# Encoder trunk in split fp32 on one core: tokens as rows in chunks 1 to 10 of each feed-forward stage, and h turned by VectorE and a trip through scratch memory

## What is computed

```python
DEPTH = 2; SEQ = 256; D_MODEL = 1024; D_FF = 2816
def _swiglu(h, w_in, w_out):
    gu = h @ w_in                       # (256, 1024) @ (1024, 5632)
    gate, up = jnp.split(gu, 2, axis=-1)
    return (jax.nn.silu(gate) * up) @ w_out
for l in range(DEPTH):
    x = x + 0.5 * _swiglu(_rmsnorm(x, ffn1_norm[l]), ffn1_w_in[l], ffn1_w_out[l])
    x = x + mixing(_rmsnorm(x, mix_norm[l]))
    x = x + 0.5 * _swiglu(_rmsnorm(x, ffn2_norm[l]), ffn2_w_in[l], ffn2_w_out[l])
```

## Time and profile before

| | |
|---|---|
| median of 3 runs | 906.71 us |
| the profiled execution | 906.24 us, span 904.4 us |
| granted TensorE clock | 1.000 of full speed throughout |
| busy share of the span | TensorE 99%, VectorE 68%, ScalarE 53%, GpSimd 6% |
| DMA | 169.63 MB, mean 188 GB/s |

### The profile page before, as it was taken

How to read it: one execution, slowest core, us unless ns; L and a number is a source line. 1 busy time by engine, 2 the same in 40 slices (tenths; PEclk the granted TensorE clock), 3 DMA queues, 4 the chain that set the end, 5 groups by cost and what they waited for, 6 DMA issues and landing times.

```text
span 904.4 us, 13686 instructions
## 1 busy us (share of the span) xinstructions
PE 899.1 (99%) x4874; PEld 765.0 (85%) x4874; DVE 615.2 (68%) x798; ACT 481.7 (53%) x602; POOL 51.7 (6%) x115
## 2 busy tenths in 40 slices
PE   9999999999999999999999999999999999999998
PEld 7888888887788888888888888888877888888887
DVE  5676656687976765665776666667789667566564
ACT  6455455467855554544555545535677455454451
POOL 4100001012100000000020000000210000000000
PEclk9999999999999999999999999999999999999999
DMA  9766666754185656455567555564532756645631
GB/s 309 206 236 198 220 205 197 224 177 139 63 274 156 214 186 227 148 201 213 163 137 266 182 205 191 185 210 162 186 134 90 245 162 216 230 147 204 208 139 47
DMA packets 123652, 169.63 MB, mean 188 GB/s; under 512 B 7284, under 2 KB 102328, under 8 KB 123616
## 3 DMA queue, kind: packets, MB, share of 16 engines
q1 hardware_dynamic: 120416, 165.57, 54.4%
q0 software_dynamic: 1296, 2.92, 2.4%
q10 hardware_dynamic: 1904, 0.67, 0.5%
HBM read 166.76 MB, written 2.36 MB: 187 GB/s over the span
## 4 chain that ended last, share of the span: by engine, by line
PE 93%; DVE 5%; ACT 1%; issue 1%; DMA 0%; ACTq 0%; SPq 0%; POOL 0%; DVEq 0%; POOLq 0%
PE TR L1344 16%; PE U L1344 16%; PE TR L1352 8%; PE U L1352 8%; PE C L1208 6%; PE C L1211 6%; PE C L1209 6%; PE D L1209 5%; PE D L1211 5%; PE D L1208 5%; PE U L1208 2%; PE U L1211 2%; PE U L1209 2%; DVE sc L1057 1%; PE TR L1248 1%; DVE w_lo L827 1%
## 5 line engine op out<-in xcount | busy, mean ns | idle before, releaser
L827 DVE TENSOR_TENSOR w_lo<-raw,w_hi 128x2048 fp32r<-128x2048 f32 x150 | 340.3, 2288 | 103.2 <-ACT w_hi L543 103.0
L543 ACT ACTIVATE w_hi<-raw 128x2048 fp32r<-128x2048 f32 x150 | 282.1, 1905 | 23.2 <-DMA raw<-in_ffn_w_in_dram 15.8
L1344 PE MATMUL U<-xT,w_hi 128*128 128x512 f32 x640 | 167.3, 392 | 0.0
L1344 PE MATMUL TR<-xT,w_hi 128*128 128x512 f32 x640 | 165.9, 391 | 0.0
L1344 PEld LDWEIGHTS TR<-xT,w_hi 128*128 128x128 f32 x640 | 119.2, 188 | 21.5
L1344 PEld LDWEIGHTS U<-xT,w_hi 128*128 128x128 f32 x640 | 115.1, 189 | 19.6
L567 ACT ACTIVATE small<-U 128x512 f32<-128x512 f32 x40 | 23.9, 598 | 152.9 <-PE U L1344 149.4
L1352 PEld LDWEIGHTS U<-xT,w_lo 128*128 128x128 f32 x640 | 86.9, 189 | 6.5
L1352 PEld LDWEIGHTS TR<-xT,w_lo 128*128 128x128 f32 x640 | 87.5, 190 | 4.3
L1352 PE MATMUL TR<-xT,w_lo 128*128 128x256 f32 x640 | 89.4, 282 | 0.0
L1352 PE MATMUL U<-xT,w_lo 128*128 128x256 f32 x640 | 88.7, 281 | 0.0
(11 more groups left out here) (165 smaller groups left out, 1117.1 us busy)
## 6 DMA issues: line engine op xcount, KB each, us to landing
raw<-in_ffn_w_in_dram SPq DMA_DIRECT2D x168, 512.0 KB, 4.8
raw<-in_ffn_w_out_dram SPq DMA_DIRECT2D x88, 512.0 KB, 4.1
raw<-in_w_mix_in_dram SPq DMA_DIRECT2D x28, 512.0 KB, 4.6
raw<-in_w_mix_out_dram SPq DMA_DIRECT2D x16, 512.0 KB, 4.2
raw<-in_ffn_w_in_dram SPq DMA_DIRECT2D x16, 256.0 KB, 4.6
bias<-bias_rows POOLq DMA_DIRECT2D x8, 192.0 KB, 5.4
xs<-in_x_dram SPq DMA_DIRECT2D x2, 512.0 KB, 4.7
a_rows<-qs SPq DMA_DIRECT2D x4, 256.0 KB, 2.9
```

Source lines behind the costliest of these rows:

```text
L543: act.activation(w_hi[:, p % SLOTS, :], raw[:, p % RAW, :], ACT.Copy).then_inc(hi_ready, 1)
L827: dve.tensor_tensor(w_lo[:, p % SLOTS, :], raw[:, p % RAW, :], w_hi[:, p % SLOTS, :].bitcast(F32), ALU.subtract).then_inc(lo_ready, 1)
L1344: last = pe.matmul(to, w_hi[:, slot, cols_of(k, kk)], xT[:, k, :, :], start=k == 0, stop=k == KT - 1)
```

## The change

Chunks 1 to 10 are entered with tokens as rows, as chunk 0 was: 48 matmuls of 512 columns, even chunks into the banks U, odd ones into TR. Gate and up of 128 tokens then lie in one bank, ScalarE takes silu with the token's scale straight from PSUM, and VectorE multiplies (`multiply`); additions, scaling and the spreading of `inv` are gone. h of chunks 0 to 9 is turned by VectorE in blocks of 32x32 (`turn_h`), stored to `h_rows` (256 KB), loaded back in four DMAs, and split by `round_h` and `rest_h`. The last chunk, 10, is turned by TensorE, its second half after leave(9) of the first tokens.

On the queue of SyncE the store and the four loads of h(c-1) stand behind both loads of `w_in` for chunk c+1 and ahead of the load of `w_out` for chunk c. In stage one ScalarE takes both silus of chunk 0, and VectorE multiplies and turns, ahead of the split of the second `w_in` unit of chunk 1. At the very start of the kernel the first half of x is transposed ahead of the gains, with 5 warm-up matmuls instead of 7, and high and low parts of its first half are taken ahead of the first split.

```diff
 # SyncE
             def ffn_weights(L, f, after):
                 def chunk(c, j=0):
                     load_in(L, f, c + 1, 0, j)
                     load_in(L, f, c + 1, 1, j)
+                    store_h(L, f, c - 1, j)      # waits for h_turned
+                    load_h(L, f, c - 1, j)       # waits for h_stored, four DMAs
                     load_out(L, f, c, j)
...
+                load_out(L, f, 10)
+                if after is not None:
+                    after()
+                store_h(L, f, 9)
+                load_h(L, f, 9)
 # ScalarE
                 def chunk(c, j=0):
                     split(L, pos_in(f, c + 1, 0), j)
-                    copy_gate(L, f, c, j)
-                    silu(L, f, c, j)
-                    copy_up(L, f, c, 0, j)
+                    round_h(L, f, c - 1, j)
                     split(L, pos_in(f, c + 1, 1), j)
-                    copy_up(L, f, c, 1, j)
-                    round_h(L, f, c, 0, j)
-                    round_h(L, f, c, 1, j)
+                    silu(L, f, c, 0, j)
+                    silu(L, f, c, 1, j)
                     split(L, pos_out(f, c), j)
 # VectorE
                 def chunk(c, j=0):
                     split(L, pos_in(f, c + 1, 0), j)
-                    add_gate(L, f, c, j)
-                    scale_gate(L, f, c, j)
-                    add_up(L, f, c, 0, j)
-                    mul_up(L, f, c, 0, j)
+                    rest_h(L, f, c - 1, j)
                     split(L, pos_in(f, c + 1, 1), j)
-                    add_up(L, f, c, 1, j)
-                    mul_up(L, f, c, 1, j)
-                    rest_h(L, f, c, 0, j)
-                    rest_h(L, f, c, 1, j)
+                    multiply(L, f, c, 0, j)      # two instructions of 128x128
+                    multiply(L, f, c, 1, j)
+                    turn_h(L, f, c, j)           # 128x512
                     split(L, pos_out(f, c), j)
...
+                rest_h(L, f, 9)
+                multiply(L, f, 10, 0)
...
+                take_hT(L, f, 0)
+                multiply(L, f, 10, 1)
...
+                take_hT(L, f, 1)
                 residual(L, 2 * f, 0)
 # TensorE
+                def chunk(c, j=0):
+                    for u in range(2):
+                        for t in range(2):
+                            if c >= 2 and u == 0:
+                                pe.wait_ge(h_done, n_ffn(L, f, c - 2, t, j))
+                            enter(c, t, u, j)
+                    leave(c - 1, 0, j)           # waits for hT_lo_done of c - 1
+                    leave(c - 1, 1, j)
...
+                enter(10, 0, 0)
+                enter(10, 0, 1)
+                enter(10, 1, 0)
+                transpose_h(0)
+                enter(10, 1, 1)
                 leave(9, 0)
+                transpose_h(1)
                 leave(10, 0)
```

More of the change, by code:

```diff
@@ L187, in encoder @@
         brow = sb("brow", [NH, RELS])[:, :]
[L190 to L193, removed]
+        U = [bank("U0"), bank("U1")]
+        TR = [bank("TR0"), bank("TR1")]
+        GU = (U, TR)
         acc = [[bank("C0"), bank("C1")], [bank("D0"), bank("D1")]]
@@ L347, in parts @@
                 def parts(dst):
[L348 to L356, removed]
+                    d = dst.rearrange("p (k g n) -> p k g n", k=4, g=2)
+                    for g in range(2):
+                        cols = bass.ds(j * (2 * FC) + (g * DFF + c * FC), FC)
+                        yield d[:, :, g, :], w_in[f][bass.ds(L, 1), :, 4 * u:4 * u + 4, cols][0]
                 load(L, pos_in(f, c, u), parts, j)
@@ L439, in _ @@
                 load_in(L, 1, 0, 1)
-                ffn_weights(L, 1)
+                ffn_weights(L, 1, (lambda: load_first(L + 1, 0)) if L < DEPTH - 1 else None)
                 if L < DEPTH - 1:
-                    for u in range(2):
-                        load_first(L + 1, u)
+                    load_first(L + 1, 1)
             for t, half in ((0, 0), (0, 1), (1, 0)):
@@ L553, in split_rest, with silu @@
                 act.activation(w_hi[:, p, UNIT // 2:], raw[:, p, UNIT // 2:], ACT.Copy).then_inc(hi_ready, 1)
-            def silu_rows(L, f, t):
+            def silu(L, f, c, t, j=0):
                 if t == 0:
[L558 to L571, removed]
                     act.wait_ge(gu_ready, n_gu(L, f, c, j))
@@ L600, in sum_squares, with take_xT @@
                 act.activation(sq[:, :].bitcast(BF16), xs[:, t, :], ACT.Square, accum_out=ms[:, t:t + 1]).then_inc(ms_done, 1)
-            def take_xT(L, q, t):
-                for half in range(2):
+            def take_xT(L, q, t, halves=(0, 1)):
+                for half in halves:
                     act.wait_ge(xg_done, n_tran(L, q, t, half))
@@ L665, in ffn @@
                 split(L, pos_out(f, 10))
-                copy_gate(L, f, 10)
-                silu(L, f, 10)
-                copy_up(L, f, 10, 0)
+                round_h(L, f, 9)
+                silu(L, f, 10, 0)
                 if after is not None:
@@ L1229, in project, with sum_out @@
                 return last
-            def sum_out(L, p, t, lhs_hi, lhs_lo, start, stop, j=0, second_half=None):
+            def sum_out(L, p, t, lhs_hi, lhs_lo, start, stop, j=0):
                 split_ready(L, p, j)
                 for kk in range(2):
-                    if kk == 1 and second_half is not None:
-                        pe.wait_ge(hT_lo_done, second_half)
                     last = products([acc[t][0][:, :], acc[t][1][:, :]], lhs_hi(kk), lhs_lo(kk), p % SLOTS,
@@ L1242, in sum_out, with transpose_x @@
                 return last
-            def transpose_x(L, q, t):
-                for half in range(2):
+            def transpose_x(L, q, t, halves=(0, 1)):
+                for half in halves:
                     for i in range(4):
@@ L1335, in transpose_h @@
                     last.then_inc(hT_psum, 1)
-                def cols_of(k, kk):
-                    return slice(k * FC + kk * P, k * FC + (kk + 1) * P)
-                def long_T(c, g, kk, ks):
-                    slot, to = pos_in(f, c, g) % SLOTS, (U, TR)[g][kk]
-                    for k in ks:
-                        last = pe.matmul(to, w_hi[:, slot, cols_of(k, kk)], xT[:, k, :, :], start=k == 0,
-                                         stop=k == KT - 1)
-                    return last
@@ L1348, in short_T @@
-                def short_T(c, g, kk):
-                    slot, to = pos_in(f, c, g) % SLOTS, (U, TR)[g][kk]
-                    for k in range(KT):
-                        last = pe.matmul(to[:, 0:S], w_lo[:, slot, cols_of(k, kk)], xT_hi[:, k, :], start=False,
-                                         stop=False)
-                    return last
-                def finish_T(c, g, kk, last):
-                    if kk == 1:
-                        last.then_inc(units_used, 1)
-                    elif g == 1:
-                        last.then_inc(gu_ready, 1)
@@ L1414, in ffn @@
                 else:
[L1415 removed]
+                    enter_entry(0, 0)
                     pe.wait_ge(x_new, n_x_new(L, 2 * f - 1, 1, 1))
```

301 lines of the change are left out of this document (105 added, 196 removed).

## The result

The changed kernel takes 914.72 us (median of 4 runs, 912.73 to 915.78), the kernel before 906.62 on the same chip: 1.0086 times as long, 95% interval 1.0072 to 1.0099. It is slower by 8.1 us, 3.2 more than the 911.5 forecast, inside the range. The profiled execution of after is the longest of its four, 915.78 us, span 914.0, against 906.24 and 904.4 of before. So the traces differ by 9.6 us, and the sum of the prediction, +4.8, is to be held against that.

What follows compares the result with a forecast made beforehand. TensorE was taken to bound the kernel, busy 899.1 of 904.4 us. Terms -7.7 + 1.6 + 5.1 + 4.3 + 0.3 + 1.2 = +4.8 us on the profiled 906.24 gave 911.0, forecast 911.5 us, range 899 to 934.

Steps and rivals of the forecast that it cites:

- the loop: 32 loop chunks: TensorE's period falls from 16.56 to 16.32 us by a shorter enter, -7.7 us.
- Rival 3: Enter: the 48 matmuls take the old enter's 11.12 us, so no -7.7; 919 us; chance 0.03.
- Chunk 10: Last chunk of each stage: shorter enter plus four transposes of h, +0.41 us a stage, +1.6 for four.
- The wait for silu and multiply: Chunk 10: first transposes wait 0.3 us for silu and multiply behind the rounding of h(9), +1.2 us for four.
- stages two to four: Their starts: TensorE waits 2.7, 1.9 and 2.7 us at leave(0) for h(0); +5.1 us with the shorter chunk 1.
- The store: Trip of h: the 256 KB store lands 4.8 us after issue, from 2.1 to 5, behind a weight unit.
- The loads: Trip of h: four loads, the last landing 2.9 us after its issue, 4.45 us in all.
- Stage one: Its start: h(0)'s store waits behind a w_in load, so leave(0) begins 4.3 us later than before.
- The start: Start of the kernel: first halves earlier, first split later; +0.3 us, from -0.5 to +1.
- Rival 1: Loop: rounding, split, multiply, turn and trip outlast TensorE's period; 916 to 945 us, most likely 930; chance 0.32.
- the forecast's slack of 0.37 us a round: Loop: a round from rounding to rounding of h takes 15.95 us, 0.37 under TensorE's 16.32; 3 us by chunk 9.
- Rival 2: Trip of h: store lands in 3.7 or 2.1 us, stalls of stages two to four vanish; 901 us; chance 0.18.

Runs made afterwards that it cites:

- one with it fallen behind the loads: Kernel after the change, but GpSimd's 31 small copies into brow wait until VectorE has made its sixth split; 912.48 us (one run).
- the bias run: Kernel after the change, but GpSimd stores bias_rows only when TensorE is through leave(2), its eight loads two chunks later; 912.51 us, ratio 1.0061.
- the run with the trip first: Changed kernel, but store and loads of h(0) stand ahead of the second w_in load for chunk 2 on SyncE's queue; 907.46 us, ratio 0.9999.
- The doubled loads: Changed kernel, but each of the four loads of h is issued twice and rounding waits for all eight; 965.65 us (one run).
- run without the early silus: Changed kernel, but in stage one chunk 1's second w_in unit is split ahead of silu, multiply and turn for the second 128 tokens; 914.88 us, ratio 1.0087.

## Why the prediction came out as it did

**What bounds the kernel, and the loop: right.** TensorE's period is 16.32 us in every loop, from 27 matmuls of the earlier trace rows, and 32 of them gave -7.68. The rule of the Trainium skill ("TensorE: Matmul & The Clock Gate", Back-to-back issue gap), which the page gives for a single matmul in isolation and by which the old and the new enter cost the same, would have made that term zero; the row of 227 ns decided rightly. Rival 3 is out.

**Chunk 10: the transposes right, the wait not.** Net of the shorter enter the transposes cost +0.30 a stage, where 0.41 was forecast. The wait for silu and multiply (+1.2) isn't there. In stage one the rounding of h(9) and its rest end at 188.23, 4.2 us ahead of the leave at 192.44, and not 3.4. The silu starts at 187.65, beside the rest and not behind it, and the multiply ends at 188.57, 0.9 us ahead of the first transposes at 189.47. The slack is larger because the trip in the loop is shorter than forecast. In stage one the store issued at 161.52 has landed by 164.47, and rounding starts at 169.77: 8.25 us, not 9.25. Late in stages two to four the trip is 5.3 to 5.8 us.

**The store: right at the first leaves, not further on.** 4.8 us was the general figure, and the sum of stage two has 5.35 (286.45 to 291.8). Right behind a weight unit the store of h(0) took 5.3 us in stage one, 5.4 in stage two, 5.25 in stage three and 5.5 in stage four. The Trainium skill's ring order ("DMA: Bandwidth & Descriptors", Queues, rings and completion order) leaned that way. It holds only where a unit is really ahead: at 161.52 the unit had been issued 3.2 us earlier, and the store took 2.9; at 391.77 it had been issued 5.9 us earlier, and the store took 2.0. That "the unit is always there", right ahead of the store, holds for the first turns alone: the median of all 40 stores is 4.0 us.

**The loads: mis-sized, both ways.** I took 2.9 us to landing, the best of the earlier trace rows. With no other DMA of the queue under way it is 1.9, and rounding starts 3.3 us after the first issue and not 4.45. So in stages two to four the waits are 1.80, 0.76 and 1.60 us, where I had 2.7, 1.9 and 2.7. The rows of the mixing stage all had a weight unit beside them, and I took their best as the free price; it was an upper bound.

**Stage one: the step that failed.** I had the trip of h(0) with the same loads as everywhere, 4.45 us from issue to the rounding. It took 7.24 (33.63 to 40.87). The cause stands in no term of mine: GpSimd's store of `bias_rows`, which writes 8 rows of 511 numbers 16 times over, runs at that time and holds the issue of the loads on SyncE's queue. Two runs show it, one with that store put late and one with it fallen behind the loads: 3.9 and 3.8 us less wait. What is left then, 4.8 us, is less than the 6.5 of the forecast (31.6 to 38.1), since the loads are quicker here too. And it runs at that time mostly because VectorE's splits stretched GpSimd's copies from 3.97 to 10.24 us; the later start of the copies adds 1.7. In before VectorE was idle for 4.83 us while they ran. I asked what the moved work does on the queue of SyncE, and not what it does to GpSimd, whose busy share is 6%.

**The clock: a missing term.** After the waits of 8.67 and 1.80 us the leave itself took 8.45 and 7.19 us, not 5.44, +4.8 in all. The prediction priced a wait by its length. The kernel before has no wait of this kind in its stages and shows a granted clock of 1.000 throughout, so its rows could not give the price; but the sum should have had a term for it. What decides is open, and the length of the wait alone does not: after 1.60 us in stage four and 0.76 in stage three the leave took 0.2 us more, after 1.99 in stage three of the bias run and after 2.04 in stage two of the run with the trip first no more than that, but after 1.80 here and after 1.86 in stage two of the bias run 1.8 us more.

**The start: mis-sized.** +1.76 against +0.3. The new order itself costs some 0.7, the rest is one execution's DMA.

**The rivals.** Rival 1, the circle longer than the period, stayed away, at 14.8 to 15.7 in the first rounds against 16.32: in stages two to four the loads issue in 1.76 us. (Its 0.9 us of stall in three of four batches was also read too large: in before the three are 0.9, 0.8 and 0.3.) The doubled loads show that it was near in the first rounds: 1.9 us more on the trip, and it decides. Further on it was not near, for there the trip is 5.3 us and a round that nothing held would take some 11.7 (5.3 and the 6.4 of the rest, an estimate from these rounds); the forecast's slack of 0.37 us a round was far too small. Rival 2, the short trip, was half true: in the loads everywhere, in the store only late in stages two to four, where it no longer saves anything.

**In sum** the forecast's direction and place were right, with errors that cancel in part: +1.5 (start), +2.5 (stage one), +5.1 (clock), -2.7 (stages two to four), -1.6 (chunk 10), 4.7 more than forecast between the profiled executions. That the median lies only 3.2 us off is in part luck: the terms missed by some 9 us one way and some 4 the other.

## What to carry to other kernels

A detour through memory that a loop hides in full has to be priced at the loop's first turn too, where the value is wanted after half a period; keep the old way there, and take the new one from the second turn on (900.6 against 914.7 us here). When VectorE's order changes, look at which of GpSimd's instructions now run beside it and which DMAs they release, even if GpSimd is busy for 6%. And a wait of the bounding engine can cost more than its length: ask what it does to the clock of the work behind it.

## What the runs showed of the hardware

- GpSimd's copies of 8 partitions take 0.17 to 0.21 us with VectorE idle, and up to 2.26 us beside VectorE's splits of 2.29 us.
- SyncE's four load issues, 1.76 us when alone, took 5.70 us beside GpSimd's store of `bias_rows`; one of them took 2.6. In before, with the same store under way, one issue of a weight load took 3.2 us (at 27.66).
- In after a store of 256 KB landed after 5.0 to 5.9 us when the second half of a weight unit had been issued 0.5 to 0.9 us ahead of it, and after 2.0 us when it had been issued 4 us or more ahead. A load of 64 KB landed after 1.8 to 2.4 us in stages two to four, up to 7.0 beside GpSimd's store (run without the early silus).
- After waits of 2.2 to 10.7 us TensorE's next 24 matmuls took 6.9 to 8.5 us and not 5.44 (mean granted clock 0.76 and 0.63 in two windows). After waits of 1.80, 1.86 and 1.90 us they took 7.2, after others of 1.99 to 2.17 us 5.6, and after all of 0.5 to 1.77 us 5.6 at most.
